# Relative bias laid out by a reversal matmul instead of two DMA passes, and the low-rank gate projection in 16-column matmuls

## The reference, cut to what matters

```python
# relative bias: one number for each distance i + 128 - j and head
dist = i + L - j                     # i: 128 queries, j: 256 keys (previous block and own)
bias = rel_bias[t5_causal_bucket(dist)]
s = einsum(q, k2) * dh ** -0.5 + bias
s = where(valid, s, -inf)

# forget gate of GLA: rank 16
z_lr = (h @ w_in)[..., 2304:2320]    # 1024 tokens x 16
log_a = log_sigmoid(z_lr @ w_gate_up + b_gate) / 16
```

## Time and profile before

| | us |
|---|---|
| median of three runs | 1106.72 |
| the profiled execution, its own time | 1106.72 |
| its span | 1104.6 |
| around the span | 2.1 |
| PE busy | 1033.9 (94%) |
| DVE busy | 702.5 (64%) |
| ACT busy | 461.3 (42%) |
| mean granted clock of PE | 0.987 |

### The profile page before, as it was taken

How to read it: one execution, slowest core, us unless ns; L and a number is a source line. 1 busy time by engine, 2 the same in 40 slices (tenths; PEclk the granted TensorE clock), 3 DMA queues, 4 the chain that set the end, 5 groups by cost and what they waited for, 6 DMA issues and landing times.

```text
span 1104.6 us, 12675 instructions
## 1 busy us (share of the span) xinstructions
PE 1033.9 (94%) x4939; PEld 830.1 (75%) x4939; DVE 702.5 (64%) x895; ACT 461.3 (42%) x713; POOL 95.0 (9%) x120
## 2 busy tenths in 40 slices
PE   1699999989999999989999999999989999999995
PEld 1578886866666788767888888888868888888884
DVE  6766665588788443698565655645348943467567
ACT  1641001337767401575545454554334243424342
POOL 0002210022322200000000000000221000001100
PEclk9999998999999999999999999999999999999997
DMA  9919651020001432316443344316997423454623
GB/s 351 306 48 316 239 180 39 1 77 1 1 1 37 153 79 77 152 41 217 162 171 134 137 169 164 141 58 247 349 345 259 152 77 115 154 208 165 216 77 152
DMA packets 87698, 164.70 MB, mean 149 GB/s; under 512 B 15331, under 2 KB 36188, under 8 KB 87516
## 3 DMA queue, kind: packets, MB, share of 16 engines
q1 hardware_dynamic: 75788, 121.41, 31.7%
q0 software_dynamic: 11856, 42.53, 10.7%
HBM read 126.15 MB, written 39.33 MB: 150 GB/s over the span
## 4 chain that ended last, share of the span: by engine, by line
PE 78%; DVE 12%; ACT 4%; DMA 2%; issue 2%; SPq 2%; DVEq 0%; ACTq 0%
PE bank L1027 24%; PE bank L1046 24%; PE bank L780 14%; PE bank L658 10%; DMA x_in<-in_x 1%; DVE small L1336 1%; PE bank L811 1%; DVE prob L1330 1%; DVE x L1650 1%; PE bank L844 1%; DMA hid_raw<-hidden_forms 1%; DVE h_lo_T L1486 1%; ACT gla_out L1835 1%; DVE gla_out L1391 1%; DVE up_lo L1446 1%
## 5 line engine op out<-in xcount | busy, mean ns | idle before, releaser
L1046 PE MATMUL bank<-dn_hi,hid_hi 128*128 128x512 f32 x448 | 175.2, 391 | 4.3 <-DVE dn_lo L1576 4.3
L1046 PE MATMUL bank<-dn_lo,hid_hi 128*128 128x512 f32 x448 | 174.9, 390 | 0.0
L1046 PE MATMUL bank<-dn_hi,hid_lo 128*128 128x512 f32 x448 | 174.8, 390 | 0.0
L1573 DVE TENSOR_TENSOR hid_lo<-hid_raw,hid_hi 128x2048 fp32r<-128x2048 f32 x28 | 64.2, 2291 | 116.0 <-ACT hid_hi L2003 116.0
L2003 ACT ACTIVATE hid_hi<-hid_raw 128x2048 fp32r<-128x2048 f32 x28 | 53.6, 1916 | 170.4 <-PE bank L1046 153.9
L780 PE MATMUL bank<-w_hi,act_hi 128*128 128x512 f32 x256 | 103.3, 403 | 0.9 <-DVE w_lo L1111 0.9
L1027 PE MATMUL bank<-h_hi_T,up_hi 128*128 128x512 f32 x256 | 100.0, 390 | 1.6 <-DVE h_lo_T L1486 1.5
L1046 PEld LDWEIGHTS bank<-dn_hi,hid_hi 128*128 128x128 f32 x448 | 84.5, 189 | 22.4 <-DVE dn_lo L1576 4.7
L780 PE MATMUL bank<-w_lo,act_hi 128*128 128x512 f32 x256 | 100.8, 394 | 0.0
L780 PE MATMUL bank<-w_hi,act_lo 128*128 128x512 f32 x256 | 100.8, 394 | 0.0
L1446 DVE TENSOR_TENSOR up_lo<-up_raw,up_hi 128x1024 fp32r<-128x1024 f32 x48 | 58.7, 1224 | 65.4 <-ACT up_hi L1908 65.4
(11 more groups left out here) (220 smaller groups left out, 1874.7 us busy)
## 6 DMA issues: line engine op xcount, KB each, us to landing
hidden_forms<-hid SPq DMA_DIRECT2D x56, 512.0 KB, 3.1
hid_raw<-hidden_forms SPq DMA_DIRECT2D x56, 512.0 KB, 4.5
ada_w<-in_w_ada POOLq DMA_DIRECT2D x32, 512.0 KB, 6.7
up_raw<-in_w_mlp_in SPq DMA_DIRECT2D x32, 512.0 KB, 4.9
dn_ring<-in_w_mlp_out POOLq DMA_DIRECT2D x24, 512.0 KB, 4.9
raw<-in_w_in SPq DMA_DIRECT2D x36, 256.0 KB, 4.9
ada_w_first<-in_w_ada SPq DMA_DIRECT2D x8, 1024.0 KB, 10.7
dn_t<-in_w_mlp_out POOLq DMA_DIRECT2D x16, 512.0 KB, 6.4
```

Source lines behind the costliest of these rows:

```text
L1046: mm = pe.matmul(b, (hid_hi, hid_lo)[x][n % 2][:, k, t * P:(t + 1) * P], (dn_hi, dn_lo)[y][n % 2][:, k, :], start=(first and i == 0), stop ...
L1573: v.tensor_tensor(hid_lo[n % 2][:, :, :], hid_raw[n % 2][:, :, :], hid_hi[n % 2][:, :, :], ALU.subtract)\
```

## The change

Two things are changed. The 128 copies of the bias row in DRAM and the four diagonal reads are dropped. In their place one DMA reads the row with a rising shift (partition p begins at element p) into `bias_rev`, a tile in the place of `gv_tok`; this is the bias tile upside down. Four float32 matmuls with a 128 x 128 reversal matrix `rev` (a new constant input, one more 64 KB DMA) turn it over into banks 4 to 7, ahead of the V stage; four ACT copies bring it from the banks to `bias` after the gate's work (`s_gate_v` 10), ahead of the last split of g_out. DVE's gate work waits for the matmuls (`s_bias_full`), PE's `gla_scores(0)` and DVE's `scores(0, 0)` for the copies (`s_bias_read`).

The gate's projection is made in the three-matmul form of the other products: `z_hi` and `z_lo` are tiles of 16 columns, and each k-tile takes three matmuls instead of two. The result has 16 rows, and `w_gate` is loaded once.

```diff
+ return {"identity": eye, "reversal": eye[::-1].copy(), ...}
# SP
+            sp.dma_start(rev[:, :], reversal).then_inc(s_const, 16)
...
             sp.wait_ge(s_rows_out, 16)
-            one_row = bass.AP(tensor=bias_rows, offset=0, ap=[[0, P], [1, HEADS * 384]])
-            sp.dma_start(bias_copies.ap(), one_row).then_inc(s_bias, 16)
+            sp.wait_ge(s_free, G_F_FIRST[1])
+            shifted = bass.AP(tensor=bias_rows, offset=0, ap=[[1, P], [384, HEADS], [1, 2 * P]])
+            sp.dma_start(bias_rev[:, :, :], shifted).then_inc(s_bias, 16)
             for s in range(4):
                 fill(SLOT_T + s, (SLOT_T + s) % 2, wide_rows((VG0, GO0)[s // 2], s % 2))
-            sp.wait_ge(s_bias, 16)
-            sp.wait_ge(s_gate_s, 8)
-            sp.wait_ge(s_gate_v, 8)
-            for i in range(HEADS // 2):
-                falling = bass.AP(tensor=bias_copies, offset=2 * 384 * i + P - 1,
-                                  ap=[[HEADS * 384 - 1, P], [384, 2], [1, 2 * P]])
-                sp.dma_start(bias[:, 2 * PAIR_OF[i]:2 * PAIR_OF[i] + 2, :], falling).then_inc(s_bias, 16)
# PE, the gate's projection
                 for k in range(KT):
-                    pe.matmul(bank[half][0:2 * RANK, :], z_pair[:, k, :], act(0)[:, k, cols], ...)
-                    mm = pe.matmul(bank[half][0:RANK, :], z_pair[:, k, 0:RANK], act(1)[:, k, cols], ...)
+                    for a, b in ((0, 0), (0, 1), (1, 0)):
+                        mm = pe.matmul(bank[half][0:RANK, :], (z_lo if a else z_hi)[:, k, :],
+                                       act(b)[:, k, half * HALF:half * HALF + HALF], ...)
# PE, ahead of the V stage
+            pe.wait_ge(s_bias, 16)
+            pe.wait_ge(s_const, 32)
+            pe.wait_ge(s_gate_copied, 2)
+            pe.wait_ge(s_ada_col, 4)
+            pe.wait_ge(s_rows, 1)
+            for i in range(4):
+                mm = pe.matmul(bank[4 + i][:, :], rev[:, :], bias_rev[:, 2 * i:2 * i + 2, :], start=True, stop=True)
+            mm.then_inc(s_bias_full, 1)
...
             front(0, 1, first=True)
-            pe.wait_ge(s_gate_copied, 2)
-            pe.wait_ge(s_ada_col, 4)
-            pe.wait_ge(s_rows, 1)
+            pe.wait_ge(s_bias_read, 1)
             gla_scores(0, first=True)
# DVE
             v.wait_ge(s_free, G_T)
+            v.wait_ge(s_bias_full, 1)
...
-            v.wait_ge(s_bias, 16 + 64)
-            v.wait_ge(s_const, 16)
+            v.wait_ge(s_bias_read, 1)
# ACT
+            a.wait_ge(s_gate_v, 10)
+            for i in range(4):
+                pair = PAIR_OF[i]
+                ins = a.activation(bias[:, 2 * pair:2 * pair + 2, :],
+                                   bank[4 + i][:, :].rearrange("p (h k) -> p h k", h=2), ACT.Copy)
+            ins.then_inc(s_bias_read, 1)
             split_hi(SLOT_T + 3, (SLOT_T + 1) % 2, G_O)
```

More of the change, by code:

```diff
@@ L52 @@
 RANK = 16
-COPIES = 2
 GATE_NORM = 16.0
@@ L124, in constants @@
     eye = np.eye(P, dtype=np.float32)
-    return {"identity": eye, "bucket_onehot": onehot, "chunk_causal": tri}
+    return {"identity": eye, "reversal": eye[::-1].copy(), "bucket_onehot": onehot, "chunk_causal": tri}
 class Chain:
@@ L154, in build @@
 def build(nc, x, c, w_ada, b_ada, w_in, w_gate_up, b_gate, gla_norm_g, attn_sinks, rel_bias,
-          w_out, w_mlp_in, w_mlp_out, final_norm_g, identity, bucket_onehot, chunk_causal, out):
+          w_out, w_mlp_in, w_mlp_out, final_norm_g, identity, reversal, bucket_onehot, chunk_causal, out):
     x_d = x[0].rearrange("(t p) d -> p t d", p=P)
@@ L165, in build @@
     bias_rows = nc.dram_tensor("bias_rows", [HEADS, 384], F32, kind="Internal")
-    bias_copies = nc.dram_tensor("bias_copies", [P, HEADS * 384], F32, kind="Internal")
     base = DGE_SCRATCH + 128
@@ L187, in build @@
     gv_tok = at(113, "gv_tok", [NT, GLA_HEADS * DV])
+    bias_rev = at(113, "bias_rev", [HEADS, 2 * P])
     x1_nrm = (at(64, "x1_nrm0", [NT // 2, D]), at(0, "x1_nrm1", [NT // 2, D]))
@@ L236, in build @@
     z_raw = at(158, "z_raw", [KT, RANK])
-    z_pair = at(158.5, "z_pair", [KT, 2 * RANK], F32R)
+    z_hi = at(158.5, "z_hi", [KT, RANK], F32R)
+    z_lo = at(159, "z_lo", [KT, RANK], F32R)
     tmp_a = at(154, "tmp_a", [T])
@@ L256, in build @@
     small = at(220, "small", [400])
+    rev = at(219.5, "rev", [P])
     taken = [0]
@@ L300, in build @@
     s_set = sem("memsets")
+    s_bias_full, s_bias_read = sem("bias_turned"), sem("bias_read")
     s_rows_full, s_rows, s_rows_out, s_bias = (
@@ L353, in build @@
     AB_FIRST = 16 * 4 * KT // 4
-    BACK_FIRST = (32, 16 * COPIES)
+    BACK_FIRST = (32, 16)
     def up_form(f):
@@ L576, in _ @@
             pool.wait_ge(s_ada_used, 6 * KT)
-            for r in range(COPIES):
-                pool.dma_start(w_gate[r * RANK:(r + 1) * RANK, :], w_gate_up[0]).then_inc(s_wg, 16)
+            pool.dma_start(w_gate[0:RANK, :], w_gate_up[0]).then_inc(s_wg, 16)
             with nc.allow_non_contiguous_dma(reason="128 gains, one a partition"):
@@ L749, in _ @@
                 pe.wait_ge(s_free, G_Z + half - 3)
-                cols = slice(half * HALF, (half + 1) * HALF)
+                n = 0
                 for k in range(KT):
[L752 to L755, removed]
+                    for a, b in ((0, 0), (0, 1), (1, 0)):
+                        mm = pe.matmul(bank[half][0:RANK, :], (z_lo if a else z_hi)[:, k, :],
+                                       act(b)[:, k, half * HALF:half * HALF + HALF],
+                                       start=(n == 0), stop=(n == 3 * KT - 1))
+                        n += 1
                 mm.then_inc(s_full, 1)
@@ L765, in _ @@
             pe.wait_ge(s_free, G_Z + 2)
-            pe.wait_ge(s_wg, 16 * COPIES)
+            pe.wait_ge(s_wg, 16)
             for tt in range(2):
@@ L770, in _ @@
                     pe.wait_ge(s_free, G_G + i - 3)
-                    pe.matmul(bank[i][:, :], w_gate[0:COPIES * RANK, tt * P:(tt + 1) * P],
-                              z_t[0:COPIES * RANK, half * HALF:(half + 1) * HALF], start=True, stop=True).then_inc(s_full, 1)
+                    pe.matmul(bank[i][:, :], w_gate[0:RANK, tt * P:(tt + 1) * P],
+                              z_t[0:RANK, half * HALF:(half + 1) * HALF], start=True, stop=True).then_inc(s_full, 1)
+            pe.wait_ge(s_bias, 16)
[6 more added lines that the diff above has]
+            mm.then_inc(s_bias_full, 1)
             def wide_pass(s, t, b, part, last):
@@ L1239, in _ @@
                     v.wait_ge(s_zhi, 1)
-                    v.tensor_tensor(z_pair[:, :, RANK:2 * RANK], z_raw[:, :, :], z_pair[:, :, 0:RANK],
-                                    ALU.subtract).then_inc(s_zlo, 1)
+                    v.tensor_tensor(z_lo[:, :, :], z_raw[:, :, :], z_hi[:, :, :], ALU.subtract).then_inc(s_zlo, 1)
                 for half in range(2):
@@ L1251, in _ @@
                 full(G_Z + half)
-                v.tensor_copy(z_t[0:COPIES * RANK, half * HALF:(half + 1) * HALF],
-                              bank[half][0:COPIES * RANK, :]).then_inc(s_free, 1)
+                v.tensor_copy(z_t[0:RANK, half * HALF:(half + 1) * HALF], bank[half][0:RANK, :]).then_inc(s_free, 1)
             for half in range(2):
@@ L1774, in _ @@
             a.wait_ge(s_z_raw, 16)
-            a.activation(z_pair[:, :, 0:RANK], z_raw[:, :, :], ACT.Copy).then_inc(s_zhi, 1)
+            a.activation(z_hi[:, :, :], z_raw[:, :, :], ACT.Copy).then_inc(s_zhi, 1)
             def gate_copy(row, nth):
@@ L1806, in _ @@
                 a.activation(tmp_a[:, :], cum[:, tt, :], ACT.Exp, scale=1.0 / GATE_NORM).then_inc(s_gate_s, 1)
+            a.wait_ge(s_gate_v, 10)
+            for i in range(4):
+                pair = PAIR_OF[i]
+                ins = a.activation(bias[:, 2 * pair:2 * pair + 2, :],
+                                   bank[4 + i][:, :].rearrange("p (h k) -> p h k", h=2),
+                                   ACT.Copy)
+            ins.then_inc(s_bias_read, 1)
             split_hi(SLOT_T + 3, (SLOT_T + 1) % 2, G_O)
```

## The result

| | before | after |
|---|---|---|
| median of seven runs, us | 1104.18 (1102.03 to 1107.34) | 1111.3 (1108.22 to 1112.57) |
| profiled execution, us | 1106.72 | 1111.64 |
| its span, us | 1104.6 | 1109.5 |
| mean granted clock | 0.987 | 0.989 |

The ratio is 1.0055, with a 95% interval of 1.0038 to 1.0074: the change made the kernel slower by 4.2 to 8.2 us. The forecast difference of 7.15 us lies inside the interval; that the medians meet it to a tenth is luck, for the means say about 1 us less.

The account below looks back on a forecast made before the run. The prediction took PE, busy without a break from 65 to 229 us, as the bound. It added 3.71 and 3.44 us, gains 0, to 1106.72 us for 1113.9 us, 0.65% slower, range 1109 to 1119.

Parts of the forecast that it names:

- PE without cover: From 65 to 229 us PE never idles, so each instruction added there costs its full length.
- z, 3.71 us: Gate's z stage: 16 more matmuls at 0.232 us each on PE cost 3.71 us.
- Reversal, 3.44 us: Four float32 reversal matmuls, eight PE instructions at 0.43 us, cost 3.44 us; bounds 3.4 and 6.9.
- Gains 0: Removing the old bias path's DRAM copy and four diagonal reads gains 0, since nothing waited for them.
- ACT copies hidden, with 0.3 us to spare: Four ACT bank copies, about 2.1 us, fit between the gate's work and ACT's next split; cost 0.
- third rival: ACT copies are late, moving scores and split; price at most 1.8 us plus gate lateness, 1115.7 us; chance 0.04.
- The clock cancels: The 6.80 us low-clock fall from 181.90 us, costing 3.4 us, happens as before and cancels in the sum.
- first rival: Full-array reversal matmuls behind the narrow gate product keep the clock at 1.00; gain 3.4 us, 1110.5 us; chance 0.22.
- The sign that the prediction gave: Granted clock 0.50 for about 7 us between 170 and 200 us; V starting about 7 us later than 182.9.
- second rival: The z stage, all 16-column matmuls, falls to the low clock; 3.4 us more (1117.3) to 14.6 more (1128.5); chance 0.10.
- The rule of the skill: Clock drops when TensorE idles between matmul bursts; by it the gapless changed stretch would stay at the full clock.
- the two later falls: Clock falls behind stretches where PE idled 1.8 us of 3.40 and 2.4 us of 4.00; said to agree with that rule.

Follow-up runs that it names:

- e1: Kernel before with only the 16-column z stage of 48 matmuls, old bias path kept; ratio 1.0018 to the kernel before.
- e8: Kernel before with the gate product zero-padded to 128 rows, plus the 16-column z stage alone; 2.1 us more in the means than that padded kernel.
- e12: Kernel before with the gate product zero-padded to 128 rows, its two-form z stage made twice (64 matmuls); mean 5.9 us above that padded kernel.
- e2: Changed kernel with the old two-form z stage put back, so only the bias path is new; ratio 1.0024 to the kernel before.
- e9: Kernel before with the gate product zero-padded to 128 rows, plus the reversal matmuls alone; 3.2 us more in the means than that padded kernel.
- e5: Changed kernel with the four reversal matmuls made twice; 1113.79 us, ratio 1.0092 to the kernel before.
- e4: Changed kernel with the gate product zero-padded to 128 rows; 1108.74 us, ratio 1.0026 to the kernel before.
- e6: Kernel before without the 128 bias copies in DRAM, the four reads taking their bytes from x; ratio 1.0007 to the kernel before.
- e10: Kernel before with each of the four 32-row gate matmuls made twice; 1111.53 us, ratio 1.0066 to the kernel before.
- e11: Kernel before with the gate product zero-padded to 128 rows and each of its four matmuls made twice; 1107.01 us, ratio 1.0024.

## Why the prediction was right

**PE without cover.** Right. The stretch is without idle time in both kernels, and each added group, alone, doubled or on another base, lengthened the kernel by about its own length once the clock is taken out: z 3.7 (e1) and 3.1 (e8) for 3.71 us, z once more 7.0 for 7.4 (e12), the reversal 3.9 (e2), 3.1 (e9) and 3.1 (e5) for 3.44.

**z, 3.71 us.** In the trace 11.13 - 7.42 = 3.71 exactly. In the time over all executions it is 2.0 us (e1) and 2.1 us (e8), with less time at the low clock: 3.4 us less in e1, which explains the missing 1.7 us, and 1.9 us less in e8, which explains 1 us. The term was read rightly and its effect on the mean was 1.6 to 1.7 us smaller.

**Reversal, 3.44 us.** 3.43 us at the full clock (e4), 5.33 us in the profile of the changed kernel, inside the stated bounds of 3.4 and 6.9.

**Gains 0.** Right, to about 1 us: e6 for the copies, e9 for the whole path.

**ACT copies hidden, with 0.3 us to spare.** 2.07 us for 2.1 and 0.36 us to spare. The third rival did not occur.

**The clock cancels.** This was the weak step. In the two profiles it did not cancel: 3.4 us at the low clock in this stretch instead of 6.8, or half of the first rival's gain; with the 0.8 us behind V this is why the spans differ by 4.9 us. The sign that the prediction gave, 0.50 for about 7 us and V starting about 7 us later, was met by half: V started 191.56 - 182.94 = 8.6 us later, since the fall now lies before it. Over all executions the clock nearly did cancel: 23.8 and 22.6 us at the low level, or 0.6 us of price. The first rival, that the clock stays up because of the reversal matmuls, is not what happened in the profile: the fall came in the last 1 us of the narrow product before and about 1 us behind it after. That the difference of the medians fits the sum so closely, with this term off in the profiles, is luck. The second rival, a fall in z, is refuted by e4, e8 and e12, where z with 16 or 32 columns ran at 1.00.

**The rule of the skill.** That the clock drops when TensorE sits idle between bursts (the Trainium skill, "TensorE: Matmul & The Clock Gate", "Why this matters for your kernels") is not enough for this kernel: e10 shows a fall without any idle time, e11 shows none with the same instructions over 128 rows. The agreement that the prediction found at the two later falls is one of direction only: the idle times there, 1.8 and 2.4 us, are shorter than the gaps that this section warns of.

## What to carry to other kernels

Where one engine is busy without a break, a DMA that lands early is free and a matmul that replaces it is not: price it at the start-to-start distance of its nearest row. Here a contraction over 32 rows cost the same PE time as one over 128 (3.62 and 3.60 us) and took the clock down in most profiles; zeros in the unused rows cost nothing that could be measured, and with them none of seven profiles showed a fall in this stretch. When executions differ by several us, compare means with the granted clock beside them before a term of 2 us is called confirmed or missing.

## What the runs showed of the hardware that was not expected

A stream of matmuls of 512 columns with 16 or 32 stationary columns over 128 rows ran at a granted clock of 1.00 for 14.8 us (e12), while in or just behind four float32 matmuls over 32 or 16 rows, with PE busy without a break, it fell to 0.50 for 6.8 us (before, e1) or 3.4 us (after), and with eight of them for 10.2 us (e10). The step depends on the execution: e2 has the same 32-row product and its profile shows no fall.
